# An S5 / RG-LRU decoder step with PEER mixers: which engine adds the rows of the second expert table, three and one or two and two

## The reference

```python
def block(args):
    xb, ib, gb = args
    u = u_emb[ib].astype(jnp.float32)
    act = jnp.einsum("nd,nhkd->nhk", xb.astype(jnp.float32), u)
    wgt = jax.nn.gelu(act, approximate=False) * gb
    v = v_emb[ib].astype(jnp.float32)
    return jnp.einsum("nhk,nhkd->nd", wgt, v)
```

## Time and profile before

| | |
|---|---|
| median of three runs | 3801.35 us (3799.45 to 3801.61) |
| profiled execution | 3798.16 us, of which the span is 3796.3 us |
| TensorE busy | 2867.0 us (76%) |
| VectorE busy | 2406.9 us (63%) |
| GpSimd busy | 1986.9 us (52%) |
| ScalarE busy | 656.7 us (17%) |
| read from HBM | 1401.86 MB, 370 GB/s over the span |
| mean granted TensorE clock | 0.89 of full speed |

### The profile page before, as it was taken

The page is one execution under the profiler, slowest core; times in us unless marked ns, Lnnn a source line. Parts: engine busy times, 40 slices in busy tenths (PEclk is TensorE's granted clock), DMA queues, the critical chain, the costliest instruction groups (busy, mean ns, idle before and its releaser), DMA issues.

```text
span 3796.3 us, 30116 instructions
## 1 busy us (share of the span) xinstructions
PE 2867.0 (76%) x10568; PEld 1645.9 (43%) x10568; DVE 2406.9 (63%) x3337; ACT 656.7 (17%) x1576; POOL 1986.9 (52%) x1620
## 2 busy tenths in 40 slices
PE   4555996777666778898986788888877687666667
PEld 2223773333222326665753456665644342222222
DVE  7997077767775555666466675665456765555563
ACT  6664021101010111221011112221010111000000
POOL 5886025566656554344465453344355556555652
PEclk8777998998888999999998889998988899888888
DMA  2001459999999999999999999999999999999997
GB/s 98 14 12 70 138 241 410 425 422 423 426 419 422 427 427 427 420 411 417 426 427 422 427 421 420 408 420 421 426 427 422 418 411 427 427 427 427 427 427 316
DMA packets 197787, 1407.03 MB, mean 371 GB/s; under 512 B 21984, under 2 KB 26336, under 8 KB 26864
## 3 DMA queue, kind: packets, MB, share of 16 engines
q0 software_dynamic: 166064, 1208.62, 76.2%
q1 hardware_dynamic: 31296, 196.39, 12.6%
q10 hardware_dynamic: 288, 0.18, 0.0%
HBM read 1401.86 MB, written 3.24 MB: 370 GB/s over the span
## 4 chain that ended last, share of the span: by engine, by line
DMA 41%; PE 25%; POOL 15%; DVE 11%; issue 6%; ACT 2%; POOLq 0%; ACTq 0%; DVEq 0%
DMA arena<-in_v_dram,arena 25%; PE ps L704 16%; DMA arena<-in_u_dram,arena 11%; PE ps L626 7%; POOL arena L567 5%; DMA W<-in_slabs_dram 5%; POOL arena L556 4%; DVE arena L1532 3%; POOL arena L494 1%; POOL arena L496 1%; DVE X L1564 1%; POOL arena L472 1%; POOL arena L500 1%; PE ps L716 1%; DVE arena L1443 1%
## 5 line engine op out<-in xcount | busy, mean ns | idle before, releaser
L704 PE MATMUL ps<-arena 128*128 128x512 f32 x3584 | 1805.1, 661 | 650.8 <-DMA arena<-in_v_dram,arena 490.3
L1532 DVE CUSTOM_DVE_ANT_0 arena<-arena,HN 128x2048 f32<-128x2048 f32 x576 | 1311.1, 2291 | 1082.5 <-DMA arena<-in_u_dram,arena 1082.3
L567 POOL DMA_INDIRECT arena<-in_v_dram,arena x576 | 870.2, 1511 | 1202.4 <-PE ps L704 861.1
L704 PEld LDWEIGHTS ps<-arena 128*128 128x128 f32 x3584 | 736.3, 212 | 1686.6 <-issue 939.1
L556 POOL DMA_INDIRECT arena<-in_u_dram,arena x576 | 838.4, 1456 | 505.6 <-DVE arena L1532 192.6
L626 PE MATMUL ps<-HT,W 128*128 128x160 f32 (+2 forms) x3520 | 515.1, 309 | 42.6 <-DMA W<-in_slabs_dram 42.2
L626 PEld LDWEIGHTS ps<-HT,W 128*128 128x128 f32 x3520 | 483.0, 196 | 83.3 <-DMA W<-in_slabs_dram 47.7
L1095 ACT ACTIVATE arena<-arena 128x4 f32<-128x4 f32 x144 | 29.6, 205 | 2026.8 <-DVE arena L1532 2026.7
L1564 DVE SCALAR_TENSOR_TENSOR X<-arena,X 128x2048 f32<-128x2048 f32 x128 | 300.9, 2351 | 69.7 <-DMA arena<-in_v_dram,arena 39.3
L626 PE MATMUL ps<-arena,W 128*128 128x160 f32 (+2 forms) x1440 | 238.8, 329 | 18.0 <-DMA W<-in_slabs_dram 18.0
L626 PEld LDWEIGHTS ps<-arena,W 128*128 128x128 f32 x1440 | 213.7, 197 | 46.4 <-DMA W<-in_slabs_dram 19.9
(11 more groups left out here) (230 smaller groups left out, 1937.2 us busy)
## 6 DMA issues: line engine op xcount, KB each, us to landing
W<-in_slabs_dram SPq DMA_DIRECT2D x168, 1024.0 KB, 10.1
arena<-in_u_dram,arena POOLq DMA_INDIRECT x576, 15.0
arena<-in_v_dram,arena POOLq DMA_INDIRECT x576, 14.0
GB<-in_norms_dram SPq DMA_DIRECT2D x7, 1024.0 KB, 14.6
arena<-in_s_bc_dram SPq DMA_DIRECT2D x32, 128.0 KB, 2.1
X<-in_x_dram SPq DMA_DIRECT2D x3, 1024.0 KB, 7.2
GB<-in_keys_dram SPq DMA_DIRECT2D x2, 1024.0 KB, 10.5
out_y_dram<-HN SPq DMA_DIRECT2D x2, 1024.0 KB, 10.1
```

Of the source, the lines that this page charges most:

```text
L567: pool.indirect_dma_start(ring[:, HALF + r, :], None, experts_v[n // LAYER_ROUNDS], bass.IndirectOffsetOnAxis(ap=GI[:, at:at + 1], axis=0) ...
L704: mm = nc.tensor.matmul(ps[:, ACC_BANK + c, :], diag[:, slot, :], ring[:, HALF + r, BANK * c:BANK * (c + 1)], start=first and r == 0, stop ...
L1532: V.tensor_tensor_reduce(ring[:, r, :], ring[:, r, :], HN[:, tile_of(n), :], 1.0, 0.0, ALU.mult, ALU.add, A8[:, n % TURN, r:r + 1]).then_i ...
```

## The change

`rows_by_pe` gives TensorE rows 0 and 1 of each round of the prompt tiles, where it had rows 0, 1 and 2; row 2 goes to VectorE, which has row 3 already. The sample tile keeps all four rows on TensorE. There are 128 rounds of the prompt tiles.

```diff
@@ -111,7 +111,7 @@
 
 
 def rows_by_pe(n):
-    return range(HALF) if tile_of(n) == 2 else range(HALF - 1)
+    return range(HALF) if tile_of(n) == 2 else range(HALF - 2)
 
 
 MM_COUNT, ADD_COUNT = {}, {}
```

## The result

The changed kernel takes 3911.62 us in the median of five runs (3907.38 to 3913.65) against 3799.77 us for the kernel before (five runs): a ratio of 1.0286, 95% interval [1.0275, 1.0298], 112 us slower. The forecast had the sign and the mechanism, and half the size (56 us, 3854 us in all; the range ended at 3895).

A forecast was written before the change was run, and what follows sets the result against it. The prediction took DMA transfers to bound the rounds, with edits counting through the supply of issued gathers. It summed 3798.2 + 40.7 (pairs) + 19.2 (keys) + 0 (slices) - 4 (tail) = 3854.1 us, range 3785 to 3895 us.

The forecast's parts named there:

- What bounds the kernel: Rounds from 580 to 3732 us: bound by DMA transfers, 423 of 427 GB/s, some 29.5 us unused.
- The moved wait of v2: GpSimd's queue: v2 waits for VectorE's row 2 add instead of TensorE, stopping one row earlier, ahead of u3 and v3.
- worked case: One choice of pairs followed gather by gather from v2 to u1: u3 lands at 62 instead of 57.1.
- The price of a choice: Expert choices on VectorE: 3.7 us late for each of 11 pairs, 1.6 us for each of 12 keys.
- The RG-LRU slices: 1530 to 1950 and 2330 to 2740 us: lighter TensorE against later v2, taken as zero, between -8 and +20 us.
- the relief: TensorE loses 1024 of 3584 instructions, some 516 us of busy time; one row less per step helps in RG-LRU slices.
- The tail: After 3732 us: v2 no longer waits for TensorE's third row, some 4 us gained, bounds 0 and 8.
- the clock: TensorE's clock, 0.83 in quiet rounds, may fall to 0.5 with longer pauses; cost nothing, covered by the transfers.
- The rule on the shared port pair: Issues beside VectorE's adds: by it 0.94 us each and 14 us less in the sum; measured rows were used instead.
- A: Rival: the transfers hide the later v2, leaving 3794 us; chance 0.18.
- B: Rival: TensorE's third row thins the line in the RG-LRU slices, so the change is faster, 3777 us; chance 0.12.
- C: Rival: VectorE becomes the bound around choices of pairs and delays add up, 3910 us; chance 0.08.

The follow-up runs named there:

- the 24 rounds with choices: Changed kernel's two-and-two split only in 24 prompt-tile rounds whose adds meet a choice outside the RG-LRU slices, three and one elsewhere: 3890.24 us against 3800.05 us before.
- the 64 plain ones: Two-and-two split only in 64 prompt-tile rounds whose adds meet neither choices nor recurrent work, three and one elsewhere: 3801.69 us against 3800.05 us before.
- the order of the queue: Changed kernel with GpSimd issuing u3 ahead of v2 in each step: 3802.19 us against 3800.05 us for the kernel before.
- row 2 alone: Kernel before, but TensorE adds rows 0, 1 and 3 and VectorE adds only row 2: 3882.89 us against 3802.0 us.
- The work without the wait: Kernel before with one more VectorE instruction of the add's form before each add: 3832.89 us against 3802.0 us.
- the relief alone: Kernel before, with TensorE doing only one of row 2's four products for the prompt tiles, nothing moved to VectorE: 3806.29 us against 3802.0 us.
- gave 17 us in another: All u gathers issued ahead of all v: 3790.49 us for two and two, 3807.2 us for three and one, against 3801.22 us before.

## Why the prediction was right in kind and wrong in size

**What bounds the kernel:** right. The difference of the two times (112 us) is, within rounding, that of the unused DMA time, 145 - 29.5 = 115 us.

**The moved wait of v2:** right, and shown by the 24 rounds with choices (90 us) against the 64 plain ones (nothing) and by the order of the queue (110 us back). Moved alone it costs 81 us, but only 39 of them at the choices. The worked case was close in its first half: v2 stood 13.01 us, its issue ended 0.8 us behind the second add, u3 came 4.3 us late (forecast 4.9).

**The price of a choice:** the step that failed. The prediction said "from there they follow at the pace of the DMA engines", and so 3.7 us for pairs; for keys it followed v2 alone, 1.6 us. Measured in layer 0: 5.2 and 3.0 us. Against a full line the forecast had the lateness shrink from 4.9 us at u3 to 4.4 at u1 (71.3 against 66.9). It grew instead, from 4.3 us at u3 to 5.0 at u1 and 5.5 at u2, and was still 5.5 at the next u3; it had been 0.7 before the change, so this choice, the worked case of the changed kernel, costs 4.8 us. I had stopped the worked case at u1, while it was still growing. Terms: choices 40.7 + 19.2 = 60 us forecast, 56 + 14 + 15 = 85 us measured.

Why it grew is known in part only. After the wait VectorE has four dot products and two adds in a row, and in the timelines the issues end 0.8 to 0.9 us behind the end of one of these. From u3 (1097.68) to u2 (1112.71) six issues take 2.5 us each: 2.2 us between dot products, as I had taken, but 3.3 us for v0, whose issue is held through a dot product that itself waited for the late u3. That is a little over the 2.456 us that the sixteen DMA engines need for a gather, so the queue doesn't catch up; but it explains only 0.3 of the 1.2 us of growth. The rest goes with the 413 GB/s at a full DMA share behind the gap, and no run shows its cause.

**The RG-LRU slices:** taken as zero between -8 and +20 us, measured +21 (10 and 11). The count left three choices of pairs and two of keys in the second one unpriced. The first holds no choice and still loses 10 us; that the recurrent work between dots and adds holds v2 there as a choice does is argued. The relief of TensorE that I set against it is worth nothing when it is tried alone in the old order, but with v2 moved it seems to count: row 2 alone, without the relief (and with v3 waiting for TensorE), loses 45 us there. And the relief was less than forecast: 417 us of TensorE's busy time, not 516, at a lower clock (0.72 and not 0.83 in the quiet rounds).

**The tail:** -4 us forecast, none measured (52 us from step 145 to the end in both), and the quiet rounds +5. With the choices and the slices this makes up the 56 us between forecast and result: 25 + 21 + 10. The timeline of TensorE in the tail of the changed kernel:

```profile
3871.16 9.58 PE L704 MATMUL ps<-arena 128*128 128x512 f32 x16 [4.23 <-DMA arena<-in_v_dram,arena]
...
3883.03 8.78 PE L704 MATMUL ps<-arena 128*128 128x512 f32 x16 [2.28 <-DMA arena<-in_v_dram,arena]
```

Two rows take up to 9.6 us, hardly less than the 10.5 us forecast for three: with pauses between them the granted clock was 0.76 (0.87 before). So the clock, which I had costed at nothing under the cover of the transfers, probably took back the gain of the tail, where the transfers give no cover; no run tried this. The +5 us of the quiet rounds, at an unchanged 427 GB/s, isn't settled. The work without the wait has it too (+6), so it seems to go with the second add; part may be only where the last mark falls, behind two adds.

**The rule on the shared port pair** (the Trainium skill, SBUF — State Buffer, section "Who interferes with whom"). The page infers that descriptor generation is not held up by a VectorE instruction that takes only the pair's read interface. By it, as the prediction applied it, issues beside adds would be free. For these gathers, which also read their indices from on-chip memory, it doesn't hold: v2's issue took 3.03 us and ended 0.8 us behind the end of the two adds (1091.72 + 4.84). Had it held, the prediction's own estimate would have been a smaller loss, not a larger one.

**The rivals:** A is refuted (387 GB/s in layer 0), B by the relief alone. C has the measured number, 3910 us, by luck, and not the mechanism: VectorE still waits for data within each pair of rounds (1.01, 1.20, 3.10 us), and the same work in another order costs nothing.

## What to carry to other kernels

In a queue that is served in order, a wait counts by its place: ask what stands behind it and how long the engine it names is away. Issue first what is released first. Here the u gathers wait for dot products, which stand ahead of the choices in VectorE's order, and the v gathers for adds, which stand behind them. Divide work between engines only after that; the same division cost 112 us in one order and gave 17 us in another. When two experiments add up to the whole loss, compare them by stage before you believe the sum. And when you work a stall through by hand, follow it until the line is as long as before, not to the first item that is late.

## What was not expected of the hardware

An indirect gather's issue took 0.94 us alone, 1.9 to 3.0 us beside VectorE's work with two inputs in on-chip memory, ending 0.8 to 0.9 us behind the instruction it met; beside a VectorE nearly without gaps GpSimd got out one gather in 2.5 us, slightly slower than the DMA engines take them (one in 2.456 us). Behind a gap in the supply the DMA engines moved 413 GB/s for 25 us at a share of 1.01, where they give 427 GB/s with a full line. A lighter TensorE fell to a lower granted clock (0.72 against 0.83 in the quiet rounds) and so gave back less time than the count of its instructions says: 29% fewer diagonal products (1024 of 3584) were 23% less busy time (1388.1 against 1805.1 us).
